# One tile of dense work per sample, prompt attention directly behind it, and 22 instead of 14 gate tiles in seven-product pairs

## What is computed

```python
z = rmsnorm(x) @ w_in        # uv, q, 3 x kv, head gates, g_a, g_b
u, v = gelu(uv)[..., :D_GM], rmsnorm(gelu(uv)[..., D_GM:], g_sgu)
q = rmsnorm(q, g_q) * HEAD_DIM ** -0.5
o_a = u * (einsum('gts,bnsgc->bntgc', tril(w_sgu), v) + b_sgu)   # 8 groups, chunks of 128
o_b = gates[0] * compressed + gates[1] * selected + gates[2] * window   # attention, 8 heads, 2 kv heads
mix = sigmoid(g_a) * (o_a @ w_proj_gmlp) + sigmoid(g_b) * (o_b @ w_proj_nsa)
x = x + mix @ w_out
y = x + square(relu(rmsnorm(x) @ w_up)) @ w_down
```

## Time and profile before

| | |
|---|---|
| median of 3 runs | 2661.26 us (2660.79 to 2662.04) |
| profiled execution | 2663.34 us, its span 2661.9 us |
| TensorE busy | 2642.8 us (99%), 21867 products |
| VectorE, ScalarE, GpSimd busy | 1938.1, 1384.3, 456.6 us |
| TensorE clock granted | 0.999 of full |

### The profile page before, as it was taken

One profiled execution on the slowest core, in us unless ns is written; L12 is line 12 of the kernel. 1 busy time (PEld: TensorE's weight loads), 2 busy tenths in 40 slices (PEclk: granted clock), 3 DMA queues, 4 the chain that ended last, 5 costly groups with the idle time before them and its releaser, 6 DMA issues. The chain is left out here.

```text
span 2661.9 us, 59475 instructions
## 1 busy us (share of the span) xinstructions
PE 2642.8 (99%) x21867; PEld 2610.6 (98%) x21867; DVE 1938.1 (73%) x3125; ACT 1384.3 (52%) x2412; POOL 456.6 (17%) x627
## 2 busy tenths in 40 slices
PE   9999999999999999999999999999999999999998
PEld 9999999999999999999999999999999999999998
DVE  6455655565557774446578888888888888988888
ACT  6435433444445452222246665666666656666656
POOL 2001232200002120013311111201212112112113
PEclk9999999999999999999999999999999999999999
DMA  6533233322224344434434656657657566566568
GB/s 220 185 96 113 86 126 110 115 89 75 76 85 142 120 157 151 136 126 136 143 108 135 160 149 172 152 153 178 149 160 178 139 166 170 142 167 161 150 165 180
DMA packets 124068, 374.20 MB, mean 141 GB/s; under 512 B 14050, under 2 KB 15730, under 8 KB 123712
## 3 DMA queue, kind: packets, MB, share of 16 engines
q1 hardware_dynamic: 69328, 245.36, 27.5%
q0 software_dynamic: 51472, 122.00, 21.5%
q10 hardware_dynamic: 3168, 5.45, 0.6%
HBM read 288.05 MB, written 91.00 MB: 142 GB/s over the span
## 5 line engine op out<-in xcount | busy, mean ns | idle before, releaser
L1953 DVE TENSOR_TENSOR w_lo<-w_raw,w_hi 128x512 fp32r<-128x512 f32 x336 | 240.6, 717 | 462.3 <-ACT w_hi L1435 461.7
L2591 DVE TENSOR_TENSOR w_lo<-w_raw,w_hi 128x1024 fp32r<-128x1024 f32 x352 | 430.1, 1224 | 107.5 <-ACT w_hi L1778 106.2
L1435 ACT ACTIVATE w_hi<-w_raw 128x512 fp32r<-128x512 f32 x336 | 210.8, 629 | 531.1 <-PE mm L879 511.6
L1778 ACT ACTIVATE w_hi<-w_raw 128x1024 fp32r<-128x1024 f32 x352 | 370.7, 1062 | 204.3 <-PE aux L1294 58.2
L879 PE MATMUL mm<-a_hi,w_hi 128*128 128x260 f32 x2176 | 449.8, 288 | 0.0
L879 PE MATMUL mm<-a_hi,w_lo 128*128 128x260 f32 x2176 | 437.9, 283 | 0.0
L879 PE MATMUL mm<-a_lo,w_hi 128*128 128x260 f32 x2176 | 437.1, 282 | 0.0
L1294 PE MATMUL aux<-at_t,w_hi 128*128 128x260 f32 x2304 | 417.4, 283 | 0.5 <-DVE w_lo L2591 0.2
L1294 PEld LDWEIGHTS aux<-at_t,w_hi 128*128 128x128 f32 x2304 | 354.8, 188 | 1.9 <-issue 1.4
L1354 PE MATMUL aux<-fb_mid,w_hi 128*128 128x260 f32 x1920 | 352.1, 283 | 1.4 <-DVE w_lo L2591 1.1
L879 PEld LDWEIGHTS mm<-a_hi,w_hi 128*128 128x128 f32 x2176 | 335.2, 188 | 6.4 <-issue 5.1
(11 more groups left out here) (461 smaller groups left out, 5302.6 us busy)
## 6 DMA issues: line engine op xcount, KB each, us to landing
w_raw<-in_w_ff SPq DMA_DIRECT2D x256, 512.0 KB, 3.8
w_raw<-in_w SPq DMA_DIRECT2D x170, 512.0 KB, 3.8
out_y_t<-y_mid POOLq DMA_DIRECT2D x120, 520.0 KB, 8.2
w_raw<-in_w_st SPq DMA_DIRECT2D x28, 512.0 KB, 3.7
g_in<-merge_d POOLq DMA_DIRECT2D x16, 520.0 KB, 5.1
merge_d<-z POOLq DMA_DIRECT2D x26, 260.0 KB, 2.4
st_f<-in_x_t POOLq DMA_DIRECT2D x16, 260.0 KB, 3.3
pages<-in_cache_cmp POOLq DMA_DIRECT2D x16, 256.0 KB, 3.2
```

Of the source, the lines that this page charges most:

```text
L1435: run(w_hi[:, c, :], raw(u, c), ACT.Copy).then_inc(hi_split, 1)
L1778: run(hi_of(p, k), source(p, k), ACT.Copy).then_inc(ff_hi, 1)
L1953: dve.tensor_tensor(w_lo[:, c, :], raw(u, c), w_hi[:, c, :].bitcast(F32), ALU.subtract).then_inc(lo_split, 1)
L2591: dve.tensor_tensor(lo_of(p, k), source(p, k), hi_of(p, k).bitcast(F32), ALU.subtract).then_inc(ff_lo, 1)
```

## The change

- A sample has one dense tile instead of two: tiles 0 to 8 carry the eight samples, each spread over two tiles (keys turned in tile i, scores in tile i+1). ScalarE takes over the copy of the window keys from VectorE. The order of the hooks is changed, and values are turned ahead of the next sample's keys, behind the softmax's maxima.
- Prompt attention follows directly, beside the last 7 of the 16 v and u tiles and 9 of the gate tiles. Groups are mixed in its last 8 units, one in each. v's norm stands beside unit 7.
- One dense tile without attention is left. Direct gate tiles are 10 instead of 18, pairs 11 instead of 7.
- The inputs of the pairs are loaded as one piece of 520 KB a slice, and prepared beside the last four attention units and the one tile; the ring has four slots for all pairs but the last.
- Loops are written out on all engines.

```diff
-N_ST = 7
+N_ST = 11
+N_SMP = DEC + 1
+N_ATT = 2 * NH
+RING, RING_END = (0, 1, 2, 3, 0, 1, 2), (0, 1, 2, 0, 1, 2, 1)
@@ TensorE
-            smp_pair(0, [lambda: norm_sum(n_norm_q(NH - 1)), turn_windows, None,
-                         lambda: (smp_values(0)(), smp_turn_keys(0)())])
-            with pe.Fori(1, DEC - 1) as b:
-                smp_pair(b, [lambda: smp_attend(b), lambda: (smp_pick(b), smp_values(b)()), smp_turn_keys(b)])
+            dense(0, [lambda: norm_sum(n_norm_q(NH - 1)), turn_windows, lambda: smp_turn_keys(0)])
+            dense(1, [lambda: smp_scores(0), lambda: (smp_values(0), smp_turn_keys(1)), lambda: smp_turn_probs(0),
+                      lambda: smp_attend(1)])
+            for i in range(2, DEC):
+                dense(i, [lambda: (smp_pick(i - 1), smp_scores(i - 1)), lambda: (smp_values(i - 1), smp_turn_keys(i)),
+                          lambda: smp_turn_probs(i - 1), lambda: smp_attend(i)])
...
+            for a in range(N_ATT // 2):
+                dense(N_SMP + a, [None, None, lambda: turn_probs(a), lambda: attend(a)], lambda: scores(a))
+            for a in range(N_ATT // 2, N_ATT):
+                i = a - N_ATT // 2
+                dense(N_SMP + a, [lambda: turn_group(i), lambda: mix_group(i), lambda: turn_probs(a),
+                                  lambda: attend(a)], lambda: scores(a))
+            dense(N_SMP + N_ATT)
@@ VectorE, samples
+            for i in range(2, DEC):
+                beside(host(i), [lambda: (smp_softmax(i - 1), smp_result(i - 1), smp_divide(i - 1)),
+                                 lambda: (smp_keys_in(i), smp_values_in(i - 1)),
+                                 lambda: (smp_probs_out(i - 1), smp_copies(i), smp_norms(i + 1) if i + 1 < DEC else None)],
+                       first=lambda: (smp_copy(i - 1), smp_scale_keys(i)))
+                tile_out(i)
@@ VectorE, v's norm in unit half - 1
+                if a == half - 1:
+                    second, end = (lambda: v_scaled(1, 4)), (lambda: v_scaled(6, GRP))
+                    turned.append(lambda: v_scaled(4, 6))
@@ VectorE, before the first pair
             p = Pair(0)
+            st_lo(3)
+            st_blocks(4)
+            st_lo(4)
+            st_blocks(5)
             st_blocks(6)
             st_lo(5)
             ring_in(p, 0)
             st_blocks(7)
+            ring_in(p, 1)
+            st_sums(p, 0)
+            st_sums(p, 1)
             st_lo(6)
-            st_sums(p, 0)
-            ring_in(p, 1)
-            st_sums(p, 1)
             st_lo(7)
@@ GpSimd
+            for i in range(DEC):
+                if i >= 2:
+                    pool.wait_ge(smp_out, 2 * i - 3)
+                    load_values(i - 1)
+                if i + 1 < DEC:
+                    pool.wait_ge(smp_kturned, 2 * i + 2)
+                    load_keys(i + 1)
+                if i % 2:
+                    v_squares(i // 2)
+                if i + 1 < DEC:
+                    smp_roots(i + 1)
```

More of the change, by code:

```diff
@@ L1214, in gate_unit @@
-            def gate_unit(m, p, hooks=(), first_hook=None):
-                unit((U_GATE // 2 + m, p), a_hi, a_lo, a_ready, x_need, hooks, first_hook=first_hook)
-            def head(g, h):
-                for w in range(2):
-                    other = turn_group(h) if w else None if whole(h, 0) else mix_group(h - 1)
-                    gate_unit(h, w, [None, other, turn_probs(g, h, w), attend(g, h, w)], scores(g, h, w))
-            head(0, 0)
-            with pe.Fori(1, REP) as h:
-                head(0, h)
@@ new lines, in parts @@
+            def parts(*fs):
+                return lambda: [f() for f in fs if f]
+            half = N_ATT // 2
+            for a in range(half):
+                h, w = divmod(a, 2)
+                start, second, end = None, None, None
+                turned = [lambda: probs_out(a, w)]
+                if a == 0:
+                    start = lambda: (dve.wait_ge(gates_made, 1), dve.wait_ge(mix_set, 1))
+                if a == half - 2:
+                    end = lambda: mean(N_NORM_V, D_GM)
+                if a == half - 1:
+                    second, end = (lambda: v_scaled(1, 4)), (lambda: v_scaled(6, GRP))
+                    turned.append(lambda: v_scaled(4, 6))
+                attention(a, [parts(start, lambda: divide(h, a, w), v_norm if a == half - 1 else None), second,
+                              parts(*turned), end])
@@ new lines, in _ @@
+            for a in range(half, N_ATT):
+                h, w = divmod(a, 2)
+                i = a - half
+                mixed_, turned, end = [lambda: group_mixed(i)], [lambda: probs_out(a, w)], None
+                if a == half:
+                    end = smp_gating
+                if a == N_ATT - 4:
+                    mixed_.append(lambda: st_blocks(0))
+                if a == N_ATT - 3:
+                    mixed_.append(lambda: st_lo(0))
+                if a == N_ATT - 2:
+                    end = lambda: st_blocks(1)
+                if a == N_ATT - 1:
+                    mixed_ += [lambda: st_lo(1), lambda: st_blocks(2)]
+                    turned.append(lambda: st_lo(2))
+                    end = lambda: st_blocks(3)
+                attention(a, [parts(lambda: group_in(i), lambda: divide(h, a, w)), parts(*mixed_), parts(*turned), end])
```

539 lines of the change are left out of this document (261 added, 278 removed).

## The result

The changed kernel takes 2668.72 us (median of 13 runs, 2665.0 to 2670.0) against 2661.37 for the kernel before on the same chip: ratio 1.0026, 95% interval 1.0017 to 1.0034, so +7.35 us, slower. The forecast was +3.4 us, 2664.7, with a difference under 5.3 us held likeliest; the range was 2654 to 2671.5. The profiled execution has a span of 2667.5 us and 21771 products, 96 fewer than before.

The account below looks back on a forecast made before the run. The prediction took the loop to be bound by TensorE: its number of products and its waits for other engines. Terms of -11.5, +4.4, +3.7, +2.7 and +4.1 summed to +3.4 us, 2664.7 us; range 2654 to 2671.5.

Parts of the forecast that it names:

- A: Products on TensorE: four more tile pairs go by seven products, 11.5 us less.
- B: Start of the samples: a wait of 4.9 us in the second tile plus 2.0 lower clock, less present waits: +4.4 us.
- The link that I named first: First sample's keys are turned behind the third chunk, not the second, so their loop starts late; no separate size.
- C: Samples in steady state: the keys' loop takes 16.25 us against TensorE's 15.64, 0.6 excess six times: +3.7 us.
- the keys' loop governs: Rival, chance 0.25: slower root and links make the samples' loop 17.0 us, 8.4 instead of 3.7; total 2671.4 us.
- D: v's norm beside attention unit 7: waits of 0.8 and some 2 us, without a clock drop, +2.7 us.
- the wait of 0.8 before the turning: Beside unit 7: exponentials end 3.5 us later against a slack of 2.7, so turning the probabilities waits 0.8 us.
- E: Entry of the seven-product pairs: VectorE comes free late, waits of 1.9 and 4.1 us against 1.9 before: +4.1 us.
- the waits in the second tile: Sign: a wait of 4 to 5 us before the first turning of values, with the clock below 1 behind it.
- at the entry: Sign: at the pairs' start one wait near 2 us and one near 4 us.
- the 0.6 in front of each turning of values: Sign: TensorE waits about 0.6 us in front of each turning of values in the samples.

Follow-up runs that it names:

- Experiment 4: Changed kernel with seven tile pairs by seven products instead of eleven, and 18 direct gate tiles: 2676.09 us, ratio 1.0056.
- keys_final (11): Kernel of 9 with ScalarE's guess of v's norm again ahead of attention unit 7's exponentials: 2653.65 us, ratio 0.9970.
- experiment 2: Changed kernel with a second buffer for the keys, so a sample's keys are loaded one tile earlier: 2659.26 us, ratio 0.9994.
- 8: Changed kernel with the edits of experiment 1 and experiment 2, second sample's keys loaded before the samples, their norms early in the first tile: 2656.24 us, ratio 0.9982.
- 9: Kernel of 8 with GpSimd's first root ahead of the second sample's key loads, guess of v's norm behind unit 7's exponentials: 2655.49 us, ratio 0.9978.
- experiment 1: Changed kernel with GpSimd's square and sum of the fourth v tile behind VectorE's scaling of the last sample's keys: 2664.0 us, ratio 1.0012.
- 3: Changed kernel with ScalarE's copy of the first quarter ahead of the last gate tile's tanh at the pairs' entry: 2668.97 us, ratio 1.0029.
- 6: Changed kernel with the first weight slot split ahead of the sixth to eighth operand blocks at the pairs' entry: 2668.45 us, ratio 1.0029.
- 10: Kernel of 9 with another order of work at the pairs' entry, no work taken away: 2655.72 us, ratio 0.9976.
- 12: Kernel of keys_final (11) with nine pairs instead of eleven, sums ahead of the second slot's split, copy and fourth split before the last tanh: 2649.61 us, ratio 0.9957.
- 5: Changed kernel with VectorE's softmax of the previous sample ahead of the scaling of the next one's keys: 2666.65 us, ratio 1.0021.
- 7: Changed kernel with the last two operand blocks on GpSimd, copy before the last tanh, addition ahead of the fourth sum: 2668.78 us, ratio 1.0030.

## Why it came out so

- **A, -11.5.** Right: 96 products fewer, the other pairs at 20.14 us each. Experiment 4 times the trade: 7.4 us for four pairs, because each step to more pairs takes away the tiles that the entry's preparation needs.
- **B, +4.4.** Right in size: +4.8. keys_final (11) has no such wait and serves as a measure. There the first three turnings are 12.31 and 15.72 apart, here 16.33 and 17.71 (clock 0.88): 4.0 and 2.0 longer. keys_final itself waits 1.2 us in this place (0.84 and 0.40), and before waited 2.5 in three waits: 4.0 + 2.0 + 1.2 - 2.5 (4.8 from unrounded times). The link that I named first, the late loop of one key buffer, is the smaller part. With the keys loaded long ahead the wait was still 3.58 (experiment 2), with their norms ahead too 0.4 or less (8, 9): VectorE's row makes it, though it takes the second buffer to move the norms.

```profile
305.66 1.04 PE L1096 MATMUL aux<-ident,stage 128*128 128x128 f32 x8
317.97 1.04 PE L1096 MATMUL aux<-ident,keys_odd 128*128 128x128 f32 x8
333.69 1.04 PE L1096 MATMUL aux<-ident,stage 128*128 128x128 f32 x8
...
433.71 1.12 PE L1180 MATMUL aux<-k_t,q_h 128*128 128x512 f32 x2
```

- **C, +3.7.** The term that was mis-sized: +8.2. In a quiet sample it was less than forecast, since the loop closes at 15.85 and not 16.25 us. TensorE's own pace is 15.5, so 0.35 over it a sample, where I had 0.6 over 15.64. But a loop with no slack passes every late link on: 18.75 and 19.3 us where the load took 5.4 and the scaling 4.38, each with a lower clock behind it. From the third turning to the first prompt score it is 109.81 us here and 100.02 in keys_final, 9.8 longer: 3.3, three times 0.3 to 0.4, 3.9, and 1.5 at the lower clock behind the last. Off this go 0.4 that before waited for a result and 1.2 by which TensorE's pace is quicker than the one I took: +8.2. The rival "the keys' loop governs" priced it at 8.4, by longer links in every sample; it was two links, once each. The first came at the same place in all six other kernels with one key buffer (waits of 1.3 to 1.8); the second is removed in experiment 1. B and C were to be 8.1 and are 13.0.
- **D, +2.7.** Too high, which hid a part of C's error: the wait of 0.8 before the turning didn't come, the second was 1.1 and not 2, without a lower clock. With the guess behind the exponentials it is 3.2 (9), so its new place is the better one.
- **E, +4.1.** Right in sum, and for the reason given, though one link of it was not the cause. Counted from the last tile's end at 762.96 to the second pair at 791.56 the entry takes 28.6 us for 20.14 of products: 8.5, of which 5.2 idle and 3.3 lower clock; before 3.9. That is +4.6. I held the wait before the third product to be ScalarE's two passes behind the drain. Taking one away moved the wait and no more (3); so did moving the first split (6), and a whole new order (10). With eleven pairs what is left as the cause is VectorE's work behind the last unit, which has no gap from 758.76 us on; its spreading over more tiles, with the sums ahead, took the price away (12). With seven pairs the same wait has another cause, the order (4).

The sum goes from +3.4 to +7.7 by B +0.4, C +4.5, D -1.6, E +0.5, and some 0.5 in the prompt stretch that no term had, at its start, where TensorE waits twice (0.43 and 0.27). The thought behind the forecast held: what was saved in products came back as waits, and more where the clock fell. Its size did not: the kernel came out twice as far from the one before as forecast, and slower beyond the 5.3 us that I had held likeliest. Of the signs, the waits in the second tile (4.2) and at the entry (2.4 and 2.8) came; the 0.6 in front of each turning of values did not.

What stays open: why the load issued at 341.52 took 5.4 us, and 5.1 to 5.7 in the six other kernels that issue it there. No run was made on it.

## To carry to other kernels

A loop over one buffer that closes 0.35 us behind the engine it feeds costs little in a quiet round and much at its one late link; look in it for the latest that each link can be, not its median, and buy slack (a second buffer of 4 KB per partition gave 9.5 us). Trade tiles for cheaper products only while tiles are left to hide the next stage's preparation: nine pairs beat eleven by 4.0 us, and eleven beat seven by 7.4 (seven only with one key buffer and the old order at the entry). When a step is taken out and the wait moves by one product, look at the whole row of the engine behind it: is it busy throughout, or does it idle ahead of work that could stand earlier? Here both were found, with eleven and with seven pairs.

## What the runs showed of the hardware

- Passes of GpSimd and VectorE at the same time slow each other: eight scalings of 128x128 took 4.38 us instead of 1.68 beside two passes of 128x520, three of the eight 1.1 to 1.3 us instead of 0.28, two of these ending 0.1 us behind a GpSimd pass; a GpSimd pass of 128x260 took 1.6 us beside VectorE and 0.75 otherwise. GpSimd's issue of loads beside the same scalings cost nothing (1.68 us in experiment 1).
- The granted clock fell behind waits of 4.2, 2.6, 2.4 and 1.6 us and cost 1.5 to 2.2 us each beyond the idle time (3.3 for the two at the entry); behind waits of 1.1, and of 1.5 and 1.7 us that lie a few us apart (experiment 9), it stayed at 1.00. The length of a wait alone does not tell: behind 1.3 us at 349 us (experiments 5 and 7) it went from 1.00 to 0.61 and 0.68 in 352 to 355 us.
- GpSimd's root of 128x8 took 2.04 us in most samples and 1.67 in others.
